# Norm factors as a power on GpSimd, at four places and in the finishing stage of a time mixing

## The reference

```python
def rms_norm(x, gain):            # the mean of squares over the last axis, eps 1e-6
    return x * rsqrt(mean(x * x) + eps) * gain

xp = rms_norm(h_p, norm_mix[i])                          # both layers
q = rms_norm(q, q_gain); k_s = rms_norm(...); k_w = rms_norm(...)      # layer 0, per head
kk = kk / jnp.maximum(jnp.sqrt(jnp.sum(kk * kk, axis=-1, keepdims=True)), 1e-12)   # layer 1, per head
...
mean = jnp.mean(o, axis=-1, keepdims=True)
var = jnp.mean(jnp.square(o - mean), axis=-1, keepdims=True)
o = ((o - mean) * lax.rsqrt(var + LN_X_EPS)).reshape(n, t, d) * ln_w + ln_b
o = o + (jnp.sum(hs(r) * hs(k) * r_k, axis=-1, keepdims=True) * hs(v)).reshape(n, t, d)
y = (o * g) @ wo
```

## Time and profile before

| | us |
|---|---|
| median of 3 runs | 2202.02 |
| lowest and highest run | 2201.52, 2203.72 |
| the profiled execution | 2207.73 |
| its span (first to last instruction) | 2206.0 |

### The profile page before, as it was taken

The page is one execution under the profiler, slowest core; times in us unless marked ns, Lnnn a source line. Parts: engine busy times, 40 slices in busy tenths (PEclk is TensorE's granted clock), DMA queues, the critical chain, the costliest instruction groups (busy, mean ns, idle before and its releaser), DMA issues. The chain is left out here.

```text
span 2206.0 us, 50128 instructions
## 1 busy us (share of the span) xinstructions
PE 1957.6 (89%) x22715; PEld 1786.3 (81%) x22715; DVE 870.0 (39%) x1207; ACT 644.7 (29%) x1019; POOL 704.3 (32%) x306
## 2 busy tenths in 40 slices
PE   6995896999999999996988869999755899999998
PEld 5993674668999999993877639999424899999998
DVE  2004246764430142336122045565489543023242
ACT  3221233664431232222222212222001433123221
POOL 2410001653344334421222213333452344334432
PEclk9986897999999999998878758999888999999999
DMA  7103771252343222211110000000210222222220
GB/s 215 65 1 113 277 263 59 59 171 100 138 170 130 90 96 96 94 60 58 41 68 27 14 11 3 4 4 4 102 48 0 96 89 94 96 96 86 91 74 40
DMA packets 51870, 184.37 MB, mean 84 GB/s; under 512 B 15238, under 2 KB 25378, under 8 KB 37450
## 3 DMA queue, kind: packets, MB, share of 16 engines
q1 hardware_dynamic: 51658, 181.16, 24.1%
HBM read 173.28 MB, written 16.25 MB: 86 GB/s over the span
## 5 line engine op out<-in xcount | busy, mean ns | idle before, releaser
L293 POOL TENSOR_TENSOR ws_t<-ring,ws_t 128x2048 fp32r<-128x2048 f32 x80 | 368.1, 4602 | 595.8 <-ACT ws_t L266 595.8
L249 PE MATMUL P<-hidh,ws_t 128*128 128x260 f32 x2688 | 435.9, 284 | 10.3 <-DVE hidl L306 10.3
L249 PE MATMUL P<-uh,ws_t 128*128 128x260 f32 x2560 | 417.4, 284 | 6.2 <-DVE ul L362 6.2
L249 PEld LDWEIGHTS P<-hidh,ws_t 128*128 128x128 f32 x2688 | 371.5, 189 | 11.1 <-issue 11.1
L249 PEld LDWEIGHTS P<-uh,ws_t 128*128 128x128 f32 x2560 | 354.6, 189 | 7.3 <-DVE ul L362 6.8
L249 PE MATMUL P<-hidl,ws_t 128*128 128x260 f32 x1344 | 271.5, 284 | 0.0
L249 PE MATMUL P<-ul,ws_t 128*128 128x260 f32 x1280 | 258.4, 284 | 0.0
L266 ACT ACTIVATE ws_t<-ring 128x2048 fp32r<-128x2048 f32 x80 | 152.8, 1910 | 286.4 <-PE P L249 286.4
L249 PEld LDWEIGHTS P<-hidl,ws_t 128*128 128x128 f32 x1344 | 207.8, 189 | 0.0
L249 PEld LDWEIGHTS P<-ul,ws_t 128*128 128x128 f32 x1280 | 197.8, 189 | 0.0
L1504 POOL TENSOR_SCALAR S_<-S_,st_ 128x512 f32<-128x512 f32 (+3 forms) x72 | 81.3, 1145 | 287.0 <-DVE st_ L1549 287.0
(11 more groups left out here) (347 smaller groups left out, 3007.6 us busy)
## 6 DMA issues: line engine op xcount, KB each, us to landing
ring<-in_weights SPq DMA_DIRECT2D x104, 1024.0 KB, 4.9
ring<-in_rows SPq DMA_DIRECT2D x32, 384.0 KB, 4.6
raw<-in_rows SPq DMA_DIRECT2D x32, 384.0 KB, 5.0
ring<-in_cv_slc SPq DMA_DIRECT2D x64, 128.0 KB, 2.2
full<-in_win_k SPq DMA_DIRECT2D x8, 512.0 KB, 3.9
ring<-in_win_v SPq DMA_DIRECT2D x8, 512.0 KB, 4.2
out_win_k<-in_win_k SPq DMA_DIRECT2D x8, 512.0 KB, 5.9
out_win_v<-in_win_v SPq DMA_DIRECT2D x8, 512.0 KB, 6.6
```

Of the source, the lines that this page charges most:

```text
L249: mm = pe.matmul(P[:, n // 2 % 2 * 4 + 2 * m + hf, 0:HT], w, xs[:, i * nk + k, hf * HT:(hf + 1) * HT], start=first_k and w is wh and xs is xh,
L293: pool.tensor_tensor(ws[:, u % 2, 1, :], ring[:, u % RING, :], ws[:, u % 2, 0, :].bitcast(F32), ALU.subtract).then_inc(wsplit_ready, 1)
```

## The change

At the five places the reciprocal on DVE and the root on ACT are gone. ACT scales before squaring, so that the sums are means already (not in `rates`, where no mean is wanted); DVE only adds eps (in `rates`: takes the maximum with 1e-24) out of PSUM; POOL then raises the 128 x 520 (or 20 x 520) tile in place to the power -1/2, with a column of -0.5 broadcast along the free axis as the second operand. A block at the start fills that column. The two tails keep their reciprocal and root.

```diff
+        def norm_pool(pool, i):
+            pool.wait_ge(rvar_ready, i + 1)
+            pool.tensor_tensor(rstd[:, :], rstd[:, :], minus_half[:, :].to_broadcast([128, T]), ALU.pow).then_inc(rstd_ready, 1)
...
-            step(dve.tensor_scalar(halves(rstd[:, :]), P[:, 6:8, 0:HT], 1.0 / D, EPS, ALU.mult, ALU.add))
-            dve.reciprocal(rstd[:, :], rstd[:, :]).then_inc(rvar_ready, 1)
+            dve.tensor_scalar(halves(rstd[:, :]), P[:, 6:8, 0:HT], EPS, None, ALU.add).then_inc(rvar_ready, 1)
...
-                        weight_rests(pool, units, ws)
+                        weight_rests(pool, units[0:1], ws)
+                        norm_pool(pool, i)
+                        weight_rests(pool, units[1:], ws)
+                        pool.wait_ge(zvar_ready, 1)
+                        pool.tensor_tensor(zr[:, :], zr[:, :], minus_half[0:HROWS, :].to_broadcast([HROWS, T]), ALU.pow).then_inc(zroot_ready, 1)
...
-                        weight_rests(pool, range(U_R, U_WO), ws)
+                        weight_rests(pool, [U_R], ws)
+                        norm_pool(pool, i)
+                        weight_rests(pool, range(U_R + 1, U_WO), ws)
...
+                        pool.wait_ge(kk_sum, 1)
+                        pool.tensor_tensor(inv[:, :], inv[:, :], minus_half[0:HROWS, :].to_broadcast([HROWS, T]), ALU.pow).then_inc(kk_inv, 1)
...
-                        act.wait_ge(kk_used, KC)
-                        act.activation(halves(inv[:, :]), P[0:HROWS, 4:6, 0:HT], ACT.Sqrt).then_inc(kk_root, 1)
...
-                        dve.wait_ge(kk_root, 1)
-                        step(dve.tensor_scalar(inv[:, :], inv[:, :], 1e-12, None, ALU.max))
-                        dve.reciprocal(inv[:, :], inv[:, :]).then_inc(kk_inv, 1)
+                        dve.wait_ge(kk_used, KC)
+                        dve.tensor_scalar(halves(inv[:, :]), P[0:HROWS, 4:6, 0:HT], 1e-24, None, ALU.max)\
+                           .then_inc(kk_sum, 1)
...
+                        def factor(m):
+                            pool.wait_ge(var_read, m + 1)
+                            r = rs[:, m % 2, :]
+                            pool.tensor_tensor(r, r, minus_half[:, :].to_broadcast([128, T]), ALU.pow).then_inc(n_root, 1)
+
+                        bonus_terms(0)
+                        bonus_terms(1)
+                        factor(0)
+                        bonus_terms(2)
+                        factor(1)
+                        for m in range(3, KC):
+                            bonus_terms(m)
+                            factor(m - 1)
+                        factor(KC - 1)
...
+                        def variance(m):
+                            dve.wait_ge(var_done, m + 1)
+                            dve.tensor_scalar(halves(rs[:, m % 2, :]), sums(4), 64e-5, None, ALU.add)\
+                               .then_inc(var_read, 1)
+
                         centre(0)
                         centre(1)
+                        variance(0)
                         for m in range(KC):
                             r = rs[:, m % 2, :]
-                            dve.wait_ge(var_done, m + 1)
-                            dve.tensor_scalar(halves(r), sums(4), 1.0 / HD, 64e-5, ALU.mult, ALU.add)\
-                               .then_inc(var_read, 1)
-                            dve.wait_ge(var_read, m + 1)
-                            dve.reciprocal(r, r).then_inc(n_var, 1)
                             if m + 2 < KC:
                                 centre(m + 2)
+                            if m + 1 < KC:
+                                variance(m + 1)
                             x = O[:, m, :]
                             dve.wait_ge(n_root, m + 1)
```

More of the change, by code:

```diff
@@ L149, in build @@
         full = sb(top, "full", [128, KC, T])
+        minus_half = sb(top, "minus_half", [128, 1])
         fixed_in = sem("fixed_in")
@@ L176, in build @@
         act_step = sem("act_step")
+        half_set = sem("half_set")
         state = {"split": 0, "unit": 0, "tile": 0, "norm": 0, "stage": 0, "stores": 0, "half": 0, "early": 0,
@@ L315, in norm_act @@
             for k in range(KC):
-                act.activation(dst[:, k, :], h[:, k, :], ACT.Square).then_inc(sq_ready, 1)
+                act.activation(dst[:, k, :], h[:, k, :], ACT.Square, scale=D ** -0.5).then_inc(sq_ready, 1)
             if units:
@@ L319, in norm_act @@
                     weight_head(act, u, units, ws)
-            act.wait_ge(rvar_ready, i + 1)
-            act.activation(rstd[:, :], rstd[:, :], ACT.Sqrt).then_inc(rstd_ready, 1)
             if halves_of:
@@ L724, in _ @@
                                 act.wait_ge(zsq_used, j - 1)
-                            act.activation(zsq[:, j % 2, :], Z[:, c, :], ACT.Square).then_inc(zsq_ready, 1)
-                        act.wait_ge(zvar_ready, 1)
-                        act.activation(zr[:, :], zr[:, :], ACT.Sqrt).then_inc(zroot_ready, 1)
+                            act.activation(zsq[:, j % 2, :], Z[:, c, :], ACT.Square, scale=HD ** -0.5)\
+                               .then_inc(zsq_ready, 1)
                     @block.vector
@@ L734, in _ @@
                         dve.wait_ge(zss_ready, 1)
-                        step(dve.tensor_scalar(halves(zr[:, :]), P[0:HROWS, 4:6, 0:HT], 1.0 / HD, EPS,
-                                               ALU.mult, ALU.add))
-                        dve.reciprocal(zr[:, :], zr[:, :]).then_inc(zvar_ready, 1)
+                        dve.tensor_scalar(halves(zr[:, :]), P[0:HROWS, 4:6, 0:HT], EPS, None, ALU.add)\
+                           .then_inc(zvar_ready, 1)
                         for j, c in enumerate(normed):
@@ L1767, in rates @@
                 kk_used = sem("kk_used")
-                kk_root = sem("kk_root")
+                kk_sum = sem("kk_sum")
                 kk_inv = sem("kk_inv")
@@ L2359, in output @@
                 var_read = sem("var_read")
-                n_var = sem("n_var")
                 n_root = sem("n_root")
@@ L2372, in _, with bonus_terms @@
                         step = Chain(pool, rk_step, "rk")
-                        for m in range(KC):
+                        def bonus_terms(m):
                             if m >= 3:
@@ L2421, in square @@
                                 act.wait_ge(var_done, m - 2)
-                            act.activation(csq[:, m % 3, :], O[:, m, :], ACT.Square).then_inc(csq_ready, 1)
-                        square(0)
-                        square(1)
+                            act.activation(csq[:, m % 3, :], O[:, m, :], ACT.Square, scale=HD ** -0.5)\
+                               .then_inc(csq_ready, 1)
                         for m in range(KC):
[L2427 to L2430, removed]
+                            square(m)
                     @block.vector
@@ L2479, in _ @@
                 sp.wait_ge(fixed_in, 80)
+            @block.gpsimd
+            def _(pool):
+                pool.memset(minus_half[:, :], -0.5).then_inc(half_set, 1)
+                pool.wait_ge(half_set, 1)
         layer0()
```

## The result

The changed kernel takes **3187.25 us** (median of 4 runs, 3184.59 to 3190.53) against 2201.77 (4 runs on the same chip): a ratio of 1.4481, interval 1.4452 to 1.451, or +985.5 us. The forecast was 2241, its range ended at 2350. The direction and the count of powers on the path hold, the price of one does not: **a power of 128 x 520 takes 83.4 to 83.8 us on POOL**, not 3.4.

A forecast was written before the change was run, and what follows sets the result against it. PE, busy 89%, was taken as the bound, so time changes only where it stands still. The places summed to 12X - 2.1, +39 us at X = 3.4, taking the median from 2202.0 to 2241 us, range 2196 to 2350.

The forecast's parts named there:

- the price X of a power on POOL: All five places: one power on POOL takes X = 3.4 us, between 1.05 and 7.3, whatever the partitions.
- the rival with a long piece of code: All places: a power is logarithm, product and exponential, X = 22, +262 us, 2464; chance 0.20 for X above 7.3.
- the sum on record: Whole kernel: all places together cost 12X - 2.1 us, +39 us at X = 3.4.
- X - 4.0: Head norms: PE starts at 173.51 + X instead of 177.52 us.
- X - 3.8: `rates`: PE starts at 1287.92 + X instead of 1291.69 us.
- 8X + 0.1: Finishing stage: total change over first tile, five middle tiles and last two, with PE at its quicker row.
- The term of 5.6 us for a slower PE: Finishing stage: half of 11.2 us, which six rounds would cost with PE at its slower row, 1.87 more each.
- nothing is gained by dropping reciprocal and root, since POOL's second rest covered them: First and second norm: POOL's second weight rest ends last, so each norm simply shifts by +X.
- the power of tile m+1 [...] takes the port, and DVE's next product (two SBUF inputs) waits X behind it: Finishing stage: the next tile's power shuts DVE out of SBUF for its whole length, adding X to each tile.
- 8.6 + X: Finishing stage: time per tile from gate product to gate product, against 7.60 us before.
- The port that does not bind: Norms and finishing stage: DVE not held, power cheap as a product; 5X - 15, -10 us at X = 1.05, 2192; chance 0.08.
- The second rival: Port binds at both norms, DVE passes a cheap power in the finishing stage; 5X - 7.7, about 2203 us; chance 0.12.

The follow-up runs named there:

- e4_finish: Changed kernel with reciprocal and root given back at the norms, head norms and `rates`, powers only in the finishing stage: 2862.94 us, ratio 1.3009.
- e8_wide: Kernel before, with eight buffers instead of three for POOL's bonus products and no wait for a gate product: 2202.52 us, ratio 1.0004.
- e1_cheap: Changed kernel with each power replaced by a product by a small constant, order and waits kept: 2213.27 us, ratio 1.0063 to the kernel before.
- e5_act_log: Kernel before, with the factors at all five places made on ACT by logarithm and exponential, no reciprocal or root there: 2178.77 us, ratio 0.9902.
- e7_act_log_late: `e5_act_log` with eight bonus buffers, no gate wait, and POOL's second rest at the first norm after DVE's products: 2157.14 us, 0.9799 to kernel before.

## Why the prediction was right and wrong

**The failed step is the price X of a power on POOL.** The prediction said "I take X = 3.4" and ended its bounds at 7.3, from the ratio that the reciprocal has to a plain instruction on DVE. It is 83.4: 25 times the choice, 11 times the upper bound, and four times the rival with a long piece of code (22). Put into the sum on record, 12 x 83.4 - 2.1 = +998.7 us stands against +985.5. So what put the result 946 us above the forecast is one number that no row of before could bear: both bounds came from other operations, the upper one from another engine's ratio, and it was no bound at all. The choice gave 0.20 to all of X above 7.3.

The Trainium skill ("GPSIMD Engine Reference", section "Performance versus the Vector engine") was hardly nearer: its 12 cycles per element gave the estimate of 5.2 us, a sixteenth of what was measured. The runs show 0.16 us a column, by estimate 192 cycles at that page's 1.2 GHz.

**Each place, against its term.** From the rows of before and after:

| place, stretch measured | before | after | difference | by the sum, X = 83.4 |
|---|---|---|---|---|
| first norm, start of the sum to PE | 8.46 | 91.38 | +82.9 | X = +83.4 |
| head norms, start of the sum to PE | 4.83 | 84.18 | +79.35 | X - 4.0 = +79.4 |
| second norm, start of the sum to `xx` | 10.77 | 94.14 | +83.4 | X = +83.4 |
| `rates`, start of the first pass over the key sums to PE | 4.59 | 84.18 | +79.6 | X - 3.8 = +79.6 |
| finishing, end of the first sum to the last gate's end | 58.87 | 723.1 | +664.3 | 8X + 0.1 = +667.3 |

Together +989.5, and the spans differ by 982.8; the other -6.7 us lie between the head norms and the second norm, 825.9 us before and 819.3 after, in a stretch that the change leaves alone but for one table load (what is left elsewhere cancels). That stretch differs by as much without any change: `e4_finish` and `e8_wide` have it as in the kernel before, and take 815.9 and 823.2 us for it. The term of 5.6 us for a slower PE is not seen in the total, though PE was slow; why comes below.

**At the two norms** the step "nothing is gained by dropping reciprocal and root, since POOL's second rest covered them" is shown by four runs: a product of 4.99 us behind the rest in the changed kernel and 4.97 in `e1_cheap`; the gains of only 1 us at the first norm and none at the second in `e5_act_log`; and the 3.3 us that `e7_act_log_late` got by moving the rest. The rule of the Trainium skill ("SBUF — State Buffer", section "Who interferes with whom"), that such a DVE instruction and POOL's shut each other out, agrees with these.

**In the finishing stage the size was right by another route, and in part by luck.** The step "the power of tile m+1 [...] takes the port, and DVE's next product (two SBUF inputs) waits X behind it" is wrong: that product lasts 1.43 us beside a power of 83.81, and 1.43 beside the 1.5 us product of `e1_cheap`. The last two powers show it once more (two powers in one row, the second from 2609.55 on):

```profile
2525.74 167.14 POOL L2391 TENSOR_TENSOR rs<-rs,minus_half 128x520 f32<-128x520 f32 x2 [5.99 <-DVE rs L2467]
2609.59 1.54 DVE L2483 SCALAR_TENSOR_TENSOR L<-L,vec,rs 128x520 f32<-128x520 f32 x1 [76.44 <-POOL rs L2391]
2611.17 0.76 DVE L2485 SCALAR_TENSOR_TENSOR L<-L,vec,rkv 128x520 f32<-128x520 f32 x1
...
2694.51 0.70 DVE L2488 TENSOR_TENSOR full<-L,P 128x520 f32<-128x520 f32 x1
```

The product that comes 0.04 us behind the power's start is held for 0.78 us, and the next one, 1.6 us behind it, runs beside the power at its full speed of 0.76. So the rule of the Trainium skill, as it speaks of a whole instruction, does not hold for the power. That the power reads its operand early and works on it outside SBUF would explain this; no run shows that part.

What puts one X on every round is that POOL makes the eight powers one after the other: 8X is the least that the stage can take. The forecast came to 8X too, with two powers ahead of the first gate product and one on the last two tiles; the trace has one and two.

Gate to gate is 92.46 = 83.81 + 8.65, where 8.6 + X was forecast, but the 8.65 is made of other terms. From the end of a power to the start of the next, the path is POOL's bonus products (2.4 us), which stand behind the power in its list, PE (5.45 us, 2150.58 to 2156.03), and the sum with its hand-over (0.8 us). The forecast had PE at 2.89 us, or 4.76 at the slower row, and DVE's three products on the path with 2.3; these run beside the power. So a PE that was slower in every round and products that cost nothing cancel, and the agreement to 0.1 us is luck.

**The rivals.** The port that does not bind, and the gain that this would have meant, fell with the 4.97 and 4.99 us at the norms. The second rival has its port half right (DVE gets past the power), but not its cheap power. The third had the right sign and the nearest price, 22 us for 83.4; whether the power is a logarithm, a product and an exponential no run shows. The dropped roots took seven table loads with them and two appeared, 16 before and 11 after; the one in the compression lies in the stretch that varies by 10 us between executions, where 1.28 us cannot be seen, and the last stretch, with the other, takes 493.6 us where it took 493.0.

## What to carry to other kernels

Before an operation is moved to an engine that has not run it in any trace at hand, its price there has to be measured, one instruction at a few widths; here a ratio between operations of another engine bounded nothing. An engine that is idle on average works through its list in order: the price of what is moved there falls on everything behind it in that list that others need, so look at what comes next. Here PE waited 86 us a round for bonus products behind a power; no run tried another order, and as long as POOL makes all eight powers none takes the stage below eight of them. For x to the power -1/2 here, a logarithm out of PSUM and an exponential on ACT (0.69 + 0.64 us for 128 x 520) beat both the reciprocal with a root (0.70 + 3.40 + 0.64) and the power on POOL (0.70 + 83.4), and what a reciprocal that leaves DVE is worth depends on the wait right under it: nothing at the second norm, 3.4 us at the head norms.

## What the runs showed of the hardware

POOL's power takes 0.16 us per column whatever the partitions (4, 20 or 128), the exponent (-1, -1/2, 1, 2) and the form of the exponent's operand; POOL's product of 128 x 520 with a broadcast operand takes 1.05 us. A power that runs 83.81 us delays a DVE product with two inputs in SBUF by 0.67 or 0.78 us only, and one that starts 1.6 us behind it not at all. And the granted clock of the finishing stage is lower where PE pauses more: 0.52 in the changed kernel (PE busy for 46.6 of 730 us), 0.76 before (39.9 of 71), 0.97 in `e7_act_log_late` (27.2 of 33), by the windows view:

```profile
1633.00:1666.00 33.00, 27.15 (x117) 21.86 (x116) 28.07 (x39) 15.86 (x25) 12.09 (x10) 0.97 0.00 0
```
